# The recurrence's preparation in another order: norms spread first, products of b first, k's work between the levels of the inversion

## What is computed

```python
kk = (k * k_k).reshape(B, S, H, N)
kk = kk / jnp.maximum(jnp.linalg.norm(kk, axis=-1, keepdims=True), 1e-12)
k = k * (1.0 + (a - 1.0) * k_a)
g = jax.nn.sigmoid(xg) @ g_up
# scan, state (v x k) per head, with at = -kk, bt = kk * a:
sa = jnp.einsum('bhvk,bhk->bhv', state, at)
state = state * wt[..., None, :] + sa[..., None] * bt[..., None, :] + vt[..., None] * kt[..., None, :]
y = jnp.einsum('bhvk,bhk->bhv', state, rt)
# after the scan
bonus = jnp.sum(rh * kh * r_k, axis=-1, keepdims=True)
y = (normalised y + bonus * vh) * g
```

## Time and profile before

| | us |
|---|---|
| median of 3 runs | 2133.53 |
| lowest, highest | 2128.83, 2133.59 |
| the profiled execution, its own time | 2133.12 |
| its span, first to last instruction | 2131.3 |
| TensorE busy | 2065.8 (97%) |
| VectorE, ScalarE, GpSimd busy | 1541.0, 1039.3, 377.6 |
| mean granted TensorE clock | 0.988 of full |

### The profile page before, as it was taken

How to read it: one execution, slowest core, us unless ns; L and a number is a source line. 1 busy time by engine, 2 the same in 40 slices (tenths; PEclk the granted TensorE clock), 3 DMA queues, 4 the chain that set the end, 5 groups by cost and what they waited for, 6 DMA issues and landing times.

```text
span 2131.3 us, 46981 instructions
## 1 busy us (share of the span) xinstructions
PE 2065.8 (97%) x18232; PEld 1858.1 (87%) x18232; DVE 1541.0 (72%) x2862; ACT 1039.3 (49%) x1801; POOL 377.6 (18%) x182
## 2 busy tenths in 40 slices
PE   8999999999999999999899999999999999999997
PEld 7887999999888987788698889999988889878885
DVE  5655798598888559855566558976988884698555
ACT  5544445444555445454455344454445554444443
POOL 0021699300000000000000226991000000000000
PEclk9999999999999999999999999999999999999998
DMA  6212354444444544455332133454445555445551
GB/s 268 81 63 90 130 178 178 177 156 158 177 177 177 198 178 158 166 189 196 138 139 100 43 114 126 179 190 163 158 160 177 177 177 198 175 157 178 189 191 64
DMA packets 46617, 335.04 MB, mean 157 GB/s; under 512 B 5168, under 2 KB 5296, under 8 KB 6320
## 3 DMA queue, kind: packets, MB, share of 16 engines
q1 hardware_dynamic: 46512, 333.61, 43.5%
HBM read 332.54 MB, written 1.05 MB: 157 GB/s over the span
## 4 chain that ended last, share of the span: by engine, by line
PE 84%; issue 5%; DVE 4%; POOL 4%; ACT 2%; DMA 1%; POOLq 0%; SPq 0%; ACTq 0%
PE PS L1647 33%; PE PS L1619 29%; PE PS L1293 9%; POOL low L433 3%; PE PS L1309 3%; PE PS L1636 2%; PE PS L1486 1%; PE PS L1519 1%; PE PS L1530 1%; PE PS L1633 1%; DMA ring<-in_w_slabs 1%; ACT high L457 1%; PE PS L1341 1%; PE PS L1392 0%; DVE low L796 0%
## 5 line engine op out<-in xcount | busy, mean ns | idle before, releaser
L648 ACT CAST high<-ring 128x1024 fp32r<-128x1024 f32 x512 | 535.9, 1048 | 533.3 <-PE PS L1619 416.8
L1619 PE MATMUL PS<-hTh,high 128*128 128x256 f32 x2048 | 588.6, 287 | 9.6 <-ACT GA L652 3.4
L1619 PE MATMUL PS<-hTl,high 128*128 128x256 f32 x2048 | 577.8, 282 | 0.0
L1619 PE MATMUL PS<-hTh,low 128*128 128x256 f32 x2048 | 577.3, 282 | 0.0
L1061 DVE TENSOR_TENSOR low<-ring,high 128x1024 fp32r<-128x1024 f32 x416 | 505.5, 1216 | 27.2 <-ACT high L648 18.1
L1619 PEld LDWEIGHTS PS<-hTh,high 128*128 128x128 f32 x2048 | 386.3, 189 | 13.4 <-ACT GA L652 7.3
L1619 PEld LDWEIGHTS PS<-hTl,high 128*128 128x128 f32 x2048 | 386.3, 189 | 1.2
L1619 PEld LDWEIGHTS PS<-hTh,low 128*128 128x128 f32 x2048 | 386.0, 188 | 0.0
L1647 PE MATMUL PS<-high,WH 128*128 128x512 f32 x1024 | 322.8, 396 | 0.0
L1647 PE MATMUL PS<-low,WH 128*128 128x512 f32 x1024 | 317.5, 391 | 0.0
L1647 PE MATMUL PS<-high,WL 128*128 128x512 f32 x1024 | 315.4, 389 | 0.0
(11 more groups left out here) (254 smaller groups left out, 2753.4 us busy)
## 6 DMA issues: line engine op xcount, KB each, us to landing
ring<-in_peer_slabs SPq DMA_DIRECT2D x256, 1024.0 KB, 4.8
ring<-in_w_slabs SPq DMA_DIRECT2D x58, 1024.0 KB, 4.9
xres<-in_x SPq DMA_DIRECT2D x2, 512.0 KB, 4.3
out<-obuf SPq DMA_DIRECT2D x2, 512.0 KB, 2.6
cst<-in_consts SPq DMA_DIRECT2D x1, 680.0 KB, 10.9
praw<-in_p_t SPq DMA_DIRECT2D x1, 512.0 KB, 15.5
gfin<-in_g_final SPq DMA_DIRECT2D x1, 512.0 KB, 5.7
vec<-in_vecs SPq DMA_DIRECT2D x1, 356.0 KB, 7.8
```

Of the source, the lines that this page charges most:

```text
L648: act.copy(high[:, (c0[L] + j) % DEEP], ring[:, place, half * D:(half + 1) * D]).then_inc(part_hi, 1)
L1619: ins = mm(PS[:, 6 + j % 2, 0:SEQ], u[:, b, ks], h[:, k], start=n == 0, stop=n == 3 * KT - 1)
```

## The change

- TensorE: the gate's rows leave the places around the spread and stand together behind the products of b, ahead of level 0's transposes, and go to banks 6 and 7. k's transposes and k's first products stand in level 1 between L1510 and L1519, the bonus matmuls in level 2, k's other products in level 3. All levels now use banks 0 to 3.
- VectorE: kk, bvec, the first half of ar, bt, the second half of ar, a first part of kmod, the four products of b, the first inverses; then the second part of kmod, kt, rkprod; k's masked products and the bonus go between the levels.
- VectorE makes level 0's mask for the second half of the places itself (one operation of 128x512), and inverts that half in one operation; GpSimd makes two quarters of it instead of four.
- ScalarE: gT is copied after level 0, ktok in level 1.
- Buffers: prods, winv, Mt0, rkprod and some others move, so that what now lives longer isn't overwritten.

```diff
-TOK_BANKS = (0, 6, 4)
+TOK_BANKS = (0, 4, 6)
@@ GpSimd @@
-                for g in range(4):
-                    pool.wait_ge(prod_ready, 8 * L + 2 * (g // 2) + 2)
+                for g in range(2):
+                    pool.wait_ge(prod_ready, 8 * L + 2)
                     pool.tensor_tensor(Mt[0][:, 4 * g:4 * g + 4], prods[:, 4 * g:4 * g + 4, 0], level(0, 4), ALU.mult).then_inc(mt_ready, 1)
+                pool.wait_ge(prod_ready, 8 * L + 4)
@@ ScalarE @@
-                act.wait_ge(lora_ps, 3 * L + 3)
-                act.copy(gT[:], PS[:, 2:4].rearrange("p a (b c) -> p (a b) c", b=2)).then_inc(g_ready, 1)
...
+                token_order(0)
+                token_order(1)
...
+                    if lv == 1:
+                        token_order(2)
...
                     if lv:
                         split(projection_tile(L, "out", lv - 1))
+                    else:
+                        act.wait_ge(lora_ps, 3 * L + 3)
+                        act.copy(gT[:], PS[:, 6:8].rearrange("p a (b c) -> p (a b) c", b=2)).then_inc(g_ready, 1)
@@ VectorE @@
+                dve.wait_ge(rn_ps, L + 1)
+                link(dve.tensor_tensor(kk[:], kk[:], PS[:, 6:8].rearrange("p a (b c) -> p (a b) c", b=2), ALU.mult))
+                dve.tensor_tensor(bvec[:], kk[:], avec[:], ALU.mult).then_inc(dve_step, 1)
...
+                dve.scalar_tensor_tensor(arv[:, :, 0], halves(kk), -1.0, edges[:, :, :, 0:CHUNK], ALU.mult, ALU.mult)
...
+                dve.tensor_tensor(bt[:], bvec[:], winv[:], ALU.mult).then_inc(bkt_ready, 1)
...
+                first_inverse(0)
+                dve.tensor_tensor(Mt[0][:, 8:16], prods[:, 8:16, 0], cst[:, K_LMASK:K_LMASK + CHUNK].unsqueeze(1).broadcast_to([P, 8, CHUNK]), ALU.mult).then_inc(dve_step, 1)
+                steps[0] += 1
+                first_inverse(1)
+                dve.wait_ge(dve_step, steps[0])
+                dve.tensor_tensor(XT[:, 8:16], Mt[0][:, 8:16], eye(8), ALU.add).then_inc(xm_ready, 2)
+
+                link(dve.scalar_tensor_tensor(kmod[:], kmod[:], 1.0, fm[:, 4:8], ALU.add, ALU.mult))
+                dve.tensor_tensor(kt[:], kmod[:], winv[:], ALU.mult).then_inc(bkt_ready, 1)
@@ TensorE @@
-                for t in range(2):
-                    gate_rows(t)
-
                 pe.wait_ge(knorm, L + 1)
...
+                pe.wait_ge(yTa_ready, L + 1)
                 chunk_products(0, 1)
...
+                pe.wait_ge(lora_in, 2 * (L + 1))
+                for t in range(4):
+                    dst = PS[:, 6 + t // 2, (t % 2) * SEQ:(t % 2 + 1) * SEQ]
+                    mm(dst, w[:, 512 + t * P:512 + (t + 1) * P], xg_s[:, 0], start=True, stop=False)
+                    ins = mm(dst, w[0:32, 1024 + t * P:1024 + (t + 1) * P], xg_s[0:32, 1], start=False, stop=True)
+                ins.then_inc(lora_ps, 1)
...
+                        if lv == 1:
+                            pe.wait_ge(bkt_ready, 3 * (L + 1))
+                            pe.wait_ge(g_ready, L + 1)
+                            token_order(2, kt)
+                            pe.wait_ge(tok_ready, 3 * L + 2)
+                            chunk_products(1, 0)
+                        elif lv == 2:
...
+                        elif lv == 3:
+                            pe.wait_ge(bonus_ready, L + 1)
+                            chunk_products(1, 1)
```

More of the change, by code:

```diff
@@ L1438, in _, with token_order @@
                 ins.then_inc(rn_ps, 1)
-                for t in range(2, 4):
-                    ins = gate_rows(t)
-                ins.then_inc(lora_ps, 1)
-                pe.wait_ge(gates_ready, 2 * (L + 1))
-                for n, src in enumerate((fm[:, 8:12], bt, kt)):
-                    if n == 1:
-                        pe.wait_ge(bkt_ready, 2 * L + 1)
+                def token_order(n, src):
                     for c in range(NCHUNK):
```

109 lines of the change are left out of this document (50 added, 59 removed).

## The result

| | before | changed |
|---|---|---|
| median, us | 2129.74 of 7 runs | 2139.82 of 7 runs |
| lowest, highest | 2124.95, 2133.59 | 2138.09, 2143.03 |
| profiled execution, its span | 2131.3 | 2137.7 |

The changed kernel is slower: ratio 1.0039, with a 95% interval of 1.0028 to 1.0051. In a second job the ratio was 1.0044 (1.0031 to 1.0057). The 2135.5 of the forecast was 4.3 us too low, and the median of before known then was 3.8 us above the one of 7 runs. So of a loss of 10.1 us the forecast had 2.4 (2135.5 against its own run's 2133.1). The time itself lies inside the stated range (2129.5 to 2142); why that says little stands at the end of the part on the prediction.

What follows compares the result with a forecast made beforehand. VectorE was taken to bound the stretch before level 1, TensorE the levels after. Layer 0 +0.8, layer 1 -1.1 and clock +2.8 gave +2.5 us on the profiled 2133.12, about 2135.5; range 2129.5 to 2142.

Steps and rivals of the forecast that it cites:

- Step 1: Spread of the norms starts at the power's end, at the slow clock; kk at 103.4, gain 1.4 us.
- Step 2: VectorE makes b's inputs first, done 109.3; TensorE's transposes of b take 1.2 us, its 64 products 1.92.
- step 6: TensorE's clock falls in the new pauses: one low stretch of 3.4 us, 1.4 us a layer on the path, 2.8 in all.
- Step 3: First inverses: VectorE's half mask and half inverse about 1.0 us each, ready at 116.7, 3.3 us earlier than before.
- Step 4: Gate's eight calls ahead of level 0 end at 116.45, so TensorE is late there; level 1 starts at 118.45, 3.4 us earlier.
- Step 5: Work put between levels 1 to 3 costs 2.2, 1.4 and 0.65 us, 4.25 a layer; other engines' moved work costs nothing.
- The late fetch in layer 0: Rival: slab's load under dense matmuls delays TensorE's instructions in each layer, 1.85 us each, 2137 to 2139; chance 0.17.
- a stop "gone": Before's TensorE stop of 1.85 us among layer 1's products of b was taken as absent, making layer 1 -1.1 us.
- one layer with a slow gate: Rival: gate's calls at the slow clock cost 8.7 us a layer, 2142 for one, 2150 for both; chance 0.14.

Runs made afterwards that it cites:

- kt early: Changed kernel with the second kmod step and kt moved ahead of VectorE's four products of b; ratio 1.0017, 4.0 us above before.
- the second profile: The changed kernel run again unaltered in a second job; ratio 1.0044, 8.9 us above before.
- single mends: Changed kernel with one edit each: masks after rkprod, kt ahead of products, gate's rows back, pauses filled, or one load moved; ratios 1.0013 to 1.0022.
- both mends of kt and pauses together: Changed kernel with kt ahead of the products of b and TensorE's two pauses filled with matmuls of zeros; ratio 1.0014, 2.2 us above before.
- masks later: Changed kernel with GpSimd's whole-matrix masks waiting until VectorE has finished rkprod; ratio 1.0013, 3.7 us above before.

## Why the prediction was off

**Step 1, norms first: right.** The spread starts 0.05 us after the power, kk at 102.78, which is 3.85 after the power's end (3.8 forecast).

**Step 2, products of b first: right in order, off in length.** bt ends at 107.54 and the transposes start at 107.59 (bt is 8.6 us behind the power, as forecast). But transposes and products took 1.83 and 2.98 us instead of 1.2 and 1.92; that is step 6.

**Step 3, first inverses: right in kind.** VectorE's mask of half of Mt took 1.22 and the inverse 1.22 us, against the 1.0 taken for each. XT was ready at 117.85 in layer 0, 18.9 after the power (17.1 forecast); of these 1.8 us 1.7 are there already at VectorE's first product (111.54), from the slow products ahead of it.

**Step 4, the gate sets level 0: right.** TensorE's row is the gate without idle time, and in layer 1 level 1 starts 18.87 us after the power; the forecast said 18.85. In the other three profiled layers it was 20.43 to 21.48, with the clock low behind the second pause in each.

**Step 5 failed in its last sentence.** The three insertions were priced at 2.2, 1.4 and 0.65 us. With kt early they measured 2.15 to 2.25, 1.47 and 0.4. What failed is "these cost nothing unless k's step comes after 120.5". It ended at 122.9. The prediction named the long mask that shares with VectorE, and had a row at 1.22 us for kt, but didn't put the two side by side: VectorE reaches kt at 119.6, and GpSimd starts its long masks at 118.4, as soon as its level 1 quarters are done. Step 3 had weighed just such an overlap, for the first inverses alone. This cost 1.95 and 2.1 us in level 1 (9.90 to 7.95, 10.15 to 8.05), so 4 us in all.

**Step 6, the clock: right, and about the right size.** It put one short low stretch on the path to level 1, 1.4 us a layer, on top of the slow spread that step 1 had already counted. Behind the second pause layer 0 has one of 3.4 us (108.3 to 111.7) and layer 1 none, and against the 18.85 of a fast clock level 1 starts 1.6 us later in layer 0 and not later in layer 1. In the second profile it is 2.6 and 1.6. So 1.7 and 4.2 us for both layers, and the forecast had 2.8. Its reason that small matmuls feel the clock little isn't borne out: 64 of them took 3.57 to 3.68 us instead of 2.08.

**The late fetch in layer 0 was a rival (0.17), put at 1.85 us.** It came in that layer only, 1.88 to 1.97 us plus the low clock behind it; moving the load gave 2.3 back (76.56 to 74.27 us). Before pays at the same place too, 0.80 (level 4 to 5 of layer 0 is 7.10 us, of layer 1 6.30), which the forecast didn't see. The reason given for before's stop, a slab's load shortly ahead, was right; but the forecast then asked whether a load falls under dense matmuls, and not whether a load stands where the next transfer of instructions is due.

**The account, profile against profile.** From power to yc the two layers grew by 6.85 and 0.88 us, 7.7 in all, where the forecast had 2.2 and 0.3. The 5.2 that are missing are kt's overlap (4.05), the late fetch in layer 0 (2.3), and a start of level 1 that was 1.1 us earlier in sum than forecast with the clock (20.49 and 18.87, against 20.25 twice). The two profiled executions differ by 6.7 us (2139.82 and 2133.12), since everything else together was 1 us shorter. The median of before is 3.4 below its profiled execution, which makes the 10.1.

The medians of the single mends (-4 to -7 us for one each) come together to more than the whole loss, and both mends of kt and pauses together gave hardly more than one. The profiles show why they overlap: what one mend frees ends in the next pause, or in the next late fetch. How the median gain of "masks later" (-5 to -6 us) splits up stays open: its profile shows 1.6 us in layer 1, but is of an execution 3.4 above its median.

**The choice of the profiled run.** The sum was made against one execution (2133.1) that had both a stop and 20.4 us of low clock in the two stretches; the median of 7 runs is 3.4 us below it. The second profile of before (2129.4) had 10.2 there. A forecast of a difference that leans on a stop "gone" has to ask first how much of it is in the median. The same choice made the range look better than it was. Its upper end, 2142, is 8.9 us above the run that it was worked out from, and the measured growth is 10.1 in the first job and 8.9 in the second. The time fell inside partly by luck: the range was meant for one layer with a slow gate, and what filled it was kt's overlap and a late fetch.

## What to carry to other kernels

When work moves from one engine's chain into another's, look at each moved step beside what the third engine does at that moment: a VectorE step with two inputs in SBUF next to a long GpSimd step can cost the whole of the other's instruction (kt 3.32 us instead of 1.22), and a wait of one engine for the other can be cheaper than the overlap. A pause taken away from the path is no gain if it leaves TensorE idle ahead of small matmuls; fill it or put real work there. And in long unrolled stretches of small matmuls, place the large loads by the instruction transfers in the trace: here a load that started just behind one cost nothing at it, and one that was still running when the next was due could stop the engine, by 0.56 to 2.4 us.

## What was not expected of the hardware

- A transfer of TensorE's instructions queues behind a 1 MB load: it started in the moment in which the load ended (150.08 and 150.08, 151.07 and 151.07), and TensorE went on 2.25 to 2.46 us after such a start. A load moved by 0.8 us took the stop of 1.9 away.
- TensorE's stop falls on the same matmul of the program (1870 or 1869, 10034), whatever line stands there, and the profile can name a releaser for it that was long done.
- A long overlap costs both sides: kt 3.32 for 1.23 us, two GpSimd masks 6.75 for 4.72, rkprod 3.83 to 6.46 for 1.66.
- 64 transposes of 64 x 64 take 2.08 us at the full clock and 3.57 to 3.68 at the low one. With matmuls of zeros in the pauses the clock stayed up through layer 1's stretch; in layer 0 it still fell at 97.8, one microsecond into the first filling.
